# The low part of a split weight piece, formed in two halves instead of one

## What is computed

```python
def moe_swiglu(h, w_router, w1, w3, w2):      # 8 experts, top 2, expert width 3584
    ...
    def expert_block(args):
        xb, e = args
        return (jax.nn.silu(xb @ w1[e]) * (xb @ w3[e])) @ w2[e]
```

## Time and profile before

| | before |
|---|---|
| median of 3 runs | 2175.34 us (2169.73 to 2176.59) |
| profiled execution, its own time | 2178.7 us |
| its span, first to last instruction | 2177.0 us |
| mean granted TensorE clock | 0.971 |
| PE busy | 2016.7 us (93%) |
| DVE busy | 1559.2 us (72%), 1622 instructions |
| ACT busy | 1137.9 us (52%) |
| the experts' part | from about 847 us to 2144 us of the span |

### The profile page before, as it was taken

The page is one execution under the profiler, slowest core; times in us unless marked ns, Lnnn a source line. Parts: engine busy times, 40 slices in busy tenths (PEclk is TensorE's granted clock), DMA queues, the critical chain, the costliest instruction groups (busy, mean ns, idle before and its releaser), DMA issues.

```text
span 2177.0 us, 33707 instructions
## 1 busy us (share of the span) xinstructions
PE 2016.7 (93%) x12158; PEld 1784.7 (82%) x12159; DVE 1559.2 (72%) x1622; ACT 1137.9 (52%) x1272; POOL 107.7 (5%) x105
## 2 busy tenths in 40 slices
PE   7898999999998987999999998999999988999992
PEld 6788788888877786999999876778999777999772
DVE  6765535344377656788788888787888787888886
ACT  5532433333255324555655677676555766555773
POOL 0000000000000002100100200101000101000102
PEclk9999999999999998999999999999999999999996
DMA  5311632232223113877776799998676998777993
GB/s 190 113 53 46 243 114 96 77 116 95 78 72 103 59 49 102 261 255 252 245 260 231 270 348 344 321 337 311 235 265 233 328 326 289 247 255 241 338 343 144
DMA packets 218794, 450.95 MB, mean 207 GB/s; under 512 B 13072, under 2 KB 64288, under 8 KB 218752
## 3 DMA queue, kind: packets, MB, share of 16 engines
q1 hardware_dynamic: 210256, 420.53, 56.2%
q0 software_dynamic: 8496, 29.85, 3.8%
HBM read 432.50 MB, written 17.84 MB: 207 GB/s over the span
## 4 chain that ended last, share of the span: by engine, by line
PE 56%; DVE 16%; DMA 12%; issue 7%; ACT 7%; SPq 1%; DVEq 0%; ACTq 0%; POOL 0%; POOLq 0%
PE ps L890 12%; DMA raw<-in_moe_w_dram 11%; PE ps L560 9%; PE ps L561 9%; PE ps L562 9%; PE ps L907 7%; DVE w_lo L1698 6%; PE ps L892 5%; PE ps L909 3%; ACT w_hi L1146 3%; SPq L437 1%; DVE w_lo L1286 1%; ACT w_hi L990 1%; ACT w_hi L1144 1%; DMA raw<-in_w_in_dram 1%
## 5 line engine op out<-in xcount | busy, mean ns | idle before, releaser
L1698 DVE TENSOR_TENSOR w_lo<-raw,w_hi 128x2048 fp32r<-128x2048 f32 x340 | 775.3, 2289 | 177.3 <-ACT w_hi L1146 174.8
L890 PE MATMUL ps<-xt,w_hi 128*128 128x320 f32 x1792 | 465.1, 347 | 3.9 <-DVE xt L1709 3.6
L1144 ACT ACTIVATE w_hi<-raw 128x1024 fp32r<-128x1024 f32 x340 | 358.7, 1055 | 154.4 <-DMA raw<-in_moe_w_dram 85.9
L892 PE MATMUL ps<-xt,w_lo 128*128 128x160 f32 x1792 | 424.0, 237 | 0.0
L1146 ACT ACTIVATE w_hi<-raw 128x1024 fp32r<-128x1024 f32 x340 | 358.0, 1053 | 54.7 <-DMA raw<-in_moe_w_dram 50.6
L892 PEld LDWEIGHTS ps<-xt,w_lo 128*128 128x128 f32 x1792 | 343.1, 191 | 0.1
L890 PEld LDWEIGHTS ps<-xt,w_hi 128*128 128x128 f32 x1792 | 337.1, 188 | 4.5 <-issue 4.4
L560 PE MATMUL ps<-act_hi,w_hi 128*128 128x512 f32 x608 | 240.9, 396 | 14.5 <-DVE act_lo L1324 7.3
L907 PE MATMUL ps<-ht,w_hi 128*128 128x320 f32 x896 | 237.0, 348 | 8.5 <-DVE fold L1818 8.5
L561 PE MATMUL ps<-act_lo,w_hi 128*128 128x512 f32 x608 | 238.8, 393 | 0.0
L562 PE MATMUL ps<-act_hi,w_lo 128*128 128x512 f32 x608 | 238.7, 393 | 0.0
(11 more groups left out here) (322 smaller groups left out, 3137.7 us busy)
## 6 DMA issues: line engine op xcount, KB each, us to landing
raw<-in_moe_w_dram SPq DMA_DIRECT2D x672, 512.0 KB, 3.9
raw<-in_w_in_dram SPq DMA_DIRECT2D x20, 1024.0 KB, 5.2
raw<-in_ffn_w_gate_dram SPq DMA_DIRECT2D x11, 1024.0 KB
raw<-in_ffn_w_up_dram SPq DMA_DIRECT2D x11, 1024.0 KB
raw<-in_ffn_w_down_dram SPq DMA_DIRECT2D x11, 1024.0 KB, 4.8
raw<-in_w_out_dram SPq DMA_DIRECT2D x8, 1024.0 KB, 5.0
y_rows<-mult POOLq DMA_DIRECT2D x1, 8192.0 KB, 24.5
y_rows<-yacc POOLq DMA_DIRECT2D x8, 512.0 KB, 5.0
```

Source lines behind the costliest of these rows:

```text
L890: pe.matmul(pairs_of(ps[:, bank, 0:2 * NW]), hi_[:, k % 4, f * P:(f + 1) * P], xt[:, k, :, 0:NW], start=k == 0, stop=False)
L892: last = pe.matmul(ps[:, bank, NW:2 * NW], lo_[:, k % 4, f * P:(f + 1) * P], xt[:, k, 0, 0:NW], start=False, stop=k == KT - 1)
L1144: act.activation(slot_hi[p % 6][:, 0:half], raw[:, n % 3, 0:half], ACT.Copy)
L1698: dve.tensor_tensor(slot_lo[p % 6], raw[:, n % 3, :], f32(slot_hi[p % 6]), ALU.subtract) \
```

## The change

Each `rest_ahead` becomes two subtractions of 1024 columns. The first waits for a new semaphore, `w_hi_half`, which ScalarE's first rounding of the piece signals. The second waits for `w_hi_done` as before and alone signals `w_lo_done`. Nothing else changes: the transfers, ScalarE's instructions, the matmuls and the place of each low part in VectorE's order. The low parts of the projections and of the dense layer stay whole.

```diff
+        w_hi_half = sem("w_hi_half")
...
-                act.activation(slot_hi[p % 6][:, 0:half], raw[:, n % 3, 0:half], ACT.Copy)
+                act.activation(slot_hi[p % 6][:, 0:half], raw[:, n % 3, 0:half], ACT.Copy).then_inc(w_hi_half, 1)
...
             def rest_ahead(p, at_):
-                n = MOE0 + p
+                n, half = MOE0 + p, PIECE // 2
+                dve.wait_ge(w_hi_half, p + 1 if at_ is None else at_ + (p + 1))
+                dve.tensor_tensor(slot_lo[p % 6][:, 0:half], raw[:, n % 3, 0:half], f32(slot_hi[p % 6][:, 0:half]),
+                                  ALU.subtract)
                 dve.wait_ge(w_hi_done, n + 1 if at_ is None else at_ + (n + 1))
-                dve.tensor_tensor(slot_lo[p % 6], raw[:, n % 3, :], f32(slot_hi[p % 6]), ALU.subtract) \
-                    .then_inc(w_lo_done, 1)
+                dve.tensor_tensor(slot_lo[p % 6][:, half:PIECE], raw[:, n % 3, half:PIECE],
+                                  f32(slot_hi[p % 6][:, half:PIECE]), ALU.subtract).then_inc(w_lo_done, 1)
```

## The result

The changed kernel takes **2147.48 us** (median of 6 runs, 2142.34 to 2148.56) against 2173.09 us for the kernel before, run beside it (6 runs, 2169.14 to 2178.55). The ratio is 0.9878, with a 95% interval from 0.9859 to 0.9897. The forecast was 2148 us.

What follows compares the result with a forecast made beforehand. A ring of transfer, rounding, low part and issue bounds one-block items, TensorE the turned ones. Gains of 15.0 + 5.6 + 6.4 = 27.0 us take 2178.7 to 2151.7, less 3.4 for the median: 2148 us, range 2132 to 2168.

Steps and rivals of the forecast that it cites:

- The ring: One-block items: TensorE waits for VectorE, VectorE for ScalarE, ScalarE for a transfer, SP for the low part three pieces earlier; 8.93 us a turn.
- 1.07 us for each turn: Where VectorE was waiting for ScalarE, the low part's end (w_lo_done) comes 2.29 - 1.22 = 1.07 us earlier.
- a chain turn near 8 us: Sign in the changed profile: a turn near 8 us, its transfer part growing where the DMA share nears 1.00.
- The one-block loops, 15.0 us: Loops of the four one-block items: gains of 1.7, 2.8, 6.5 and 4.0 us by using idle DMA share, together 15.0.
- 0.985: DMA share assumed for the changed one-block loops, between 0.97 of the best loop and 1.00 of the best chunk.
- The ends, 5.6 us: Ends of one-block items: low part, hidden block and TensorE's restart come sooner, 1.5 us at three ends, 1.07 at the last.
- The turned items, 6.4 us: First chunk of each of four turned items: `fold` comes about 1.8 us earlier, saving 1.6 us an item.
- The extra occupancy: On VectorE: two halves cost 0.08 us more for each piece, 27 us over 340, hidden where VectorE has room.
- The transfers were not at their limit: Rival: transfers already at their limit, loops gain nothing, 10.7 us gained in all, 2165 us; chance 0.18.
- VectorE did not set the pace: Rival, slower: VectorE sets the pace in one-block chunks, at 0.55 us more a piece 10 us lost, 2185 us; chance 0.07.
- the rival of no change: Rival: VectorE comes late to the first half in most turns that matter, within 0.3%, about 2173 us; chance 0.10.
- all the room is used: Rival: loops stop only at DMA share 1.00, ends and turned items gain fully, 41 us, 2134 us; chance 0.10.

Runs made afterwards that it cites:

- split_late: The changed kernel with both halves of the low part waiting for ScalarE's second rounding, so nothing starts early: 2186.3 us, 1.0063 of the kernel before.
- quarter_early: The changed kernel with 512 columns of the low part formed early and 1536 late: 2159.7 us, 0.9930 of the kernel before.
- before_light: The kernel before, with the second transfer of each expert piece bringing half its bytes (weights partly left out): 2144.5 us, 0.9870 of the kernel before.
- slot_by_half: The changed kernel, with SP allowed to refill a raw slot's first half once that half is subtracted: 2120.1 us, 0.9769 of the kernel before.
- after_light: The changed kernel, with the second transfer of each expert piece bringing half its bytes (weights partly left out): 2111.5 us, 0.9720 of the kernel before.
- release_only: slot_by_half with both halves of the low part formed after ScalarE's second rounding: 2180.9 us, 1.0034 of the kernel before.

## Why the prediction was right, step by step

**The mechanism: right.** The ring of transfer, rounding, low part and issue set the pace of the one-block items, and the change shortened it by starting the first half early. split_late (no early start, no gain), quarter_early (half the head start, 43% of the gain there) and before_light (the same effect from another member of the ring) show it. These are two pieces of the changed kernel on ScalarE and VectorE, in order of time.

```profile
1261.64 1.06 ACT L1145 ACTIVATE w_hi<-raw 128x1024 fp32r<-128x1024 f32 x1 [0.37 <-DMA raw<-in_moe_w_dram]
1262.89 1.06 ACT L1147 ACTIVATE w_hi<-raw 128x1024 fp32r<-128x1024 f32 x1 [0.19 <-DMA raw<-in_moe_w_dram]
```

```profile
1262.73 1.23 DVE L1699 TENSOR_TENSOR w_lo<-raw,w_hi 128x1024 fp32r<-128x1024 f32 x1
1263.98 1.23 DVE L1702 TENSOR_TENSOR w_lo<-raw,w_hi 128x1024 fp32r<-128x1024 f32 x1
```

The first half starts with the second rounding, and the second half right when that ends, at 1263.95. The low part ends 1.26 us after the rounding, where it ended 2.33 us after it.

**1.07 us for each turn: nearly.** Behind the rounding 0.91 us went (2.43 to 1.52). But the turn shortened only by 0.51 us, since the part up to the rounding grew by 0.38 and gave that much back. The forecast said in words that the transfers would give some of it back. Its sign of "a chain turn near 8 us" did not come: the mean turn is 8.93 us, and the 8.93 us that the forecast had read for the kernel before was one quick turn, where the mean was 9.44. The longest wait for `fold` is 0.8 us, where it had said under 0.6.

**The one-block loops, 15.0 us: mis-sized.** They gained 2.5, 5.1, 9.1 and 5.4 us, together 22.1. The step that failed is "One chunk ran at a DMA share of 1.00 and took 17.79 us; so the transfers cannot give a chunk in much less". A chunk of the changed kernel, cut in the same way, took 16.63 us, and slot_by_half ran whole loops at 373 GB/s. The transfers had no such limit near, and my 0.985, a guess between two shares, kept the estimate low. The limit that was near is the one that the next sentence of the forecast has and the sum did not use: TensorE's 17.2 us for a chunk. It measured 17.11 (after_light). From one chunk's first matmul to the next one's it took 18.6 us on average before and 17.5 after; cut by TensorE's work, heads and loops went from 493.7 to 466.7 us, 27 of the 36 us that lay above the floor.

**The ends, 5.6 us: mis-sized the other way.** The three ends, by the same stretches, gained 0.9, -0.3 and 0.8 us, not 4.5. Here the low part is not alone in front of TensorE's restart. These rows of the changed kernel's VectorE show such an end.

```profile
1352.23 1.23 DVE L1702 TENSOR_TENSOR w_lo<-raw,w_hi 128x1024 fp32r<-128x1024 f32 x1
1353.38 1.28 DVE L1809 TENSOR_TENSOR yacc<-yacc,ps 128x512 f32<-128x512 f32 x2
1354.57 0.68 DVE L1793 TENSOR_TENSOR ht<-ps,ht 128x512 fp32r<-128x512 f32 x1
```

The order is that of the earlier trace rows, and all of it moved forward by 3.2 us (`ht` at 1354.57, before at 1357.78). But TensorE also arrived earlier (1350.2, before at 1353.5), because the loop in front of it had become faster, and waited 5.2 us (before 5.0). Cut at TensorE's work, all four restarts gained 1.0 us (57.2 to 56.2). All one-block items together gained 549.4 - 521.5 = 27.9 us, where loops and ends of the forecast had 20.6. That the restarts could be shortened, but by more than this change, slot_by_half shows (41.5 us).

**The turned items, 6.4 us: right in size, incomplete in kind.** They gained 6.5 us: nothing in the first, 2.2 in each of the others. One of the two waits for `fold` went. (In the profiled execution of the changed kernel 3.4 us at 1.2 GHz reach into the first item; in that of the kernel before they had ended there.) But this is the difference of two larger terms, 17.6 us from the early start less 11.1 us from the split.

**The extra occupancy, "all of it where VectorE has room": wrong.** The price for each piece was right (0.07 us measured, 0.08 forecast; the 0.16 that the forecast worked out from the Trainium skill, "VectorE: DVE Perf Modes", the section on the TRN2 errata, was too much, as part of each instruction is overlapped by the next). That it costs nothing holds only as long as the early start makes up for it. Without it, it cost 11 us in the turned items of split_late and 9 in those of release_only.

**Why the total came out.** From the trace: 27.9 + 6.5 = 34.4 us less in the items. 2.9 us came back before the first item and 0.7 after the last, hence the span's 30.8 us (2177.0 to 2146.2). The part before the first item varies between executions by some us whatever the kernel (its end lies between 867.4 and 872.4 us in the profiled runs here). The profiled execution of before was also at the high end of its runs, 2178.7 us against a median of 2173. In medians the gain is 25.6 us, the forecast 27.0. Part of that agreement is luck: the loops brought more than I had allowed, the ends less, and the profiled execution overstated what there was to gain.

**The rivals.** The transfers were not at their limit. VectorE did not set the pace (97.9 of 106.5 us). The change did what it says: the part of a turn behind the rounding fell from 2.43 to 1.52 us, so the first half seldom started as late as the rival of no change had it. Room left unused by the change was there, but not of the kind in "all the room is used": 9 us in heads and loops up to TensorE's own pace, and 23 us at the restarts.

## What to carry to other kernels

Where a few buffers go round between a transfer and two engines, measure the turn (from one freeing of a buffer to the next) and take it apart; any member that can start on half of its input shortens it, and freeing the buffer by halves shortened it further here, though by itself it gave little. Do not take a high busy share of the DMA engines for a limit: take out part of the transfers once, and what is left comes near the floor. Compare two kernels over stretches that are cut at the same instructions of the engine in question, as windows cut at another engine's work can hold different amounts of it. When the loops are near their floor, look at the restarts between them. Splitting an instruction costs little, but it pays only for what it lets start early, and an engine with idle time can still have no slack in front of one particular wait.

## What was not expected of the hardware

- The 16 DMA engines moved 373 GB/s for 102 us (slot_by_half), and 376 GB/s in one chunk of the changed kernel, where the best chunk before had 350 at a share of 1.00. The share is no scale of what is left: it read 1.02 and 1.03 in these.
- PE's busy time is not the work alone. For the same 480 matmuls and 28 transposes it read 116.64 us in the kernel before, 114.82 in the changed kernel and 114.24 in slot_by_half, in stretches of 120.66, 115.17 and 114.24 us. The first of these has 3.4 us at 1.2 GHz in it.
- An instruction split in two costs VectorE 0.07 us until the next start, although the two durations add up to 0.15 us more (2 x 1.220 against 2.289).
